# Sixteen start places instead of one for the moving operand of a split float32 matmul

## The reference

```python
h = rmsnorm(r, mix_pre_g)
z = h @ w_in + b_in                       # q, k, v | f_logit | u | g_attn, g_pool
attn = forgetting_attention(q, k, v, logf)
pool = multiscale_pool(u, pool_w, pool_scale)
m = sigmoid(g_attn) * (attn @ w_attn_o) + sigmoid(g_pool) * (pool @ w_pool_o)
r = r + rmsnorm(m @ w_out, mix_post_g)
h = rmsnorm(r, ffn_pre_g)
a = causal_dwconv(h @ w_up, conv_w, conv_b)      # width 3, 2 x 5632 channels
gate, val = split(a)
r = r + rmsnorm((gelu(gate) * val) @ w_down, ffn_post_g)
return r[:, 16:]
```

## Time and profile before

| | |
|---|---|
| time, median of 3 runs | 2045.64 us (2044.01 to 2048.0) |
| the profiled execution: its own time | 2047.04 us |
| its span, first to last instruction | 2045.2 us |
| TensorE, matmuls | 2004.3 us, 98% |
| TensorE, weight loads | 1914.3 us, 94% |
| VectorE | 1288.3 us, 63% |
| ScalarE | 987.0 us, 48% |
| GpSimd | 139.7 us, 7% |
| mean granted TensorE clock | 0.988 |

### The profile page before, as it was taken

The page is one execution under the profiler, slowest core; times in us unless marked ns, Lnnn a source line. Parts: engine busy times, 40 slices in busy tenths (PEclk is TensorE's granted clock), DMA queues, the critical chain, the costliest instruction groups (busy, mean ns, idle before and its releaser), DMA issues.

```text
span 2045.2 us, 39382 instructions
## 1 busy us (share of the span) xinstructions
PE 2004.3 (98%) x15326; PEld 1914.3 (94%) x15326; DVE 1288.3 (63%) x1668; ACT 987.0 (48%) x1434; POOL 139.7 (7%) x148
## 2 busy tenths in 40 slices
PE   6999999999999999999999999999999999999998
PEld 4999999999999999999999999999999999988886
DVE  6766878775677544444447753776776677665545
ACT  3334355565645444444445444644444445444444
POOL 0000000000002000000004211000010000000000
PEclk8899999999999999999999999999999999999999
DMA  9986866565545666554544555366556655665554
GB/s 355 346 299 192 295 219 214 177 202 169 163 160 169 178 175 174 166 154 144 147 150 147 195 196 164 114 203 183 169 177 199 188 174 177 210 202 192 194 187 143
DMA packets 188103, 391.75 MB, mean 192 GB/s; under 512 B 11955, under 2 KB 17632, under 8 KB 185568
## 3 DMA queue, kind: packets, MB, share of 16 engines
q1 hardware_dynamic: 186992, 388.03, 59.2%
q10 hardware_dynamic: 1024, 2.51, 0.4%
HBM read 388.39 MB, written 2.10 MB: 191 GB/s over the span
## 4 chain that ended last, share of the span: by engine, by line
PE 91%; DVE 4%; DMA 2%; ACT 1%; issue 1%; SPq 1%; DVEq 0%; ACTq 0%
PE acc L833 21%; PE acc L835 20%; PE acc L834 20%; PE psum_y L834 2%; PE psum_x L834 2%; PE psum_y L835 2%; PE psum_x L835 2%; PE psum_x L833 2%; PE psum_y L833 2%; PE acc L1253 2%; PE acc L1255 2%; PE acc L1254 2%; DMA ada_w<-in_w_ada 1%; DVE w_lo L1851 1%; PE psum_y L1253 1%; PE psum_x L1253 1%
## 5 line engine op out<-in xcount | busy, mean ns | idle before, releaser
L1851 DVE TENSOR_TENSOR w_lo<-raw,w_hi 128x1024 fp32r<-128x1024 f32 (+1 forms) x644 | 810.6, 1272 | 634.5 <-ACT w_hi L1317 632.0
L1317 ACT ACTIVATE w_hi<-raw 128x1024 fp32r<-128x1024 f32 (+1 forms) x644 | 671.0, 1050 | 783.2 <-PE acc L835 514.6
L833 PE MATMUL acc<-act_hi,w_lo 128*128 128x258 f32 (+2 forms) x3424 | 977.1, 285 | 6.8 <-DVE act_lo L1845 1.4
L834 PE MATMUL acc<-act_lo,w_hi 128*128 128x258 f32 (+2 forms) x3424 | 965.5, 282 | 0.0
L835 PE MATMUL acc<-act_hi,w_hi 128*128 128x258 f32 (+2 forms) x3424 | 965.3, 282 | 0.0
L833 PEld LDWEIGHTS acc<-act_hi,w_lo 128*128 128x128 f32 x3424 | 648.4, 189 | 15.7 <-issue 10.6
L834 PEld LDWEIGHTS acc<-act_lo,w_hi 128*128 128x128 f32 x3424 | 648.7, 189 | 0.6 <-issue 0.5
L835 PEld LDWEIGHTS acc<-act_hi,w_hi 128*128 128x128 f32 x3424 | 648.4, 189 | 0.0
L833 PE MATMUL psum_x<-act_hi,w_lo 128*128 128x258 f32 x352 | 99.3, 282 | 0.0
L835 PE MATMUL psum_y<-act_hi,w_hi 128*128 128x258 f32 x352 | 99.1, 281 | 0.0
L834 PE MATMUL psum_y<-act_lo,w_hi 128*128 128x258 f32 x352 | 99.1, 281 | 0.0
(11 more groups left out here) (326 smaller groups left out, 2270.5 us busy)
## 6 DMA issues: line engine op xcount, KB each, us to landing
raw<-in_w_in SPq DMA_DIRECT2D x272, 512.0 KB, 3.7
raw<-in_w_ffn_up SPq DMA_DIRECT2D x176, 512.0 KB, 4.5
raw<-in_w_ffn_down SPq DMA_DIRECT2D x88, 512.0 KB, 3.6
ada_w<-in_w_ada SPq DMA_DIRECT2D x64, 512.0 KB, 9.8
raw<-in_w_out SPq DMA_DIRECT2D x64, 512.0 KB, 4.0
ada_x<-in_w_ada SPq DMA_DIRECT2D x16, 1024.0 KB, 5.7
raw<-in_w_attn_o SPq DMA_DIRECT2D x16, 512.0 KB, 3.7
raw<-in_w_pool_o SPq DMA_DIRECT2D x16, 512.0 KB, 4.6
```

The lines of the kernel that those rows point to most:

```text
L833: pe.matmul(out, w_lo, a_hi, start=c == 0, stop=False)
L834: pe.matmul(out, w_hi, a_lo, start=False, stop=False)
L1317: act.activation(M.hi[s][:, 0:job.width], M.raw[s][:, 0:job.width], ACT.Copy).then_inc(M.hi_ready[s], 1)
L1851: dve.tensor_tensor(M.lo[s][:, 0:job.width], M.raw[s][:, 0:job.width], M.hi[s][:, 0:job.width].bitcast(FP32), ALU.subtract).then_inc(M.lo_ ...
```

## The change

The distance between the chunks of `act2_hi` and `act2_lo` becomes 323 columns, 1292 bytes, where it was 320 columns, 1280 bytes. The tensors keep their places and their size of 16 x 320 columns; the last chunk ends at column 5117. All readers (the jobs) and writers (`hi2_of`, `part2_hi`, `part2_lo`) of these chunks use the new distance. Chunk 0 stays where it was.

```diff
 PITCH = 320
+STEP = 323
...
     def act2(k, c0, n):
-        return M.act2_hi[:, PITCH * k + c0:PITCH * k + c0 + n], M.act2_lo[:, PITCH * k + c0:PITCH * k + c0 + n]
+        return M.act2_hi[:, STEP * k + c0:STEP * k + c0 + n], M.act2_lo[:, STEP * k + c0:STEP * k + c0 + n]
...
     def hi2_of(k, n):
-        return M.act2_hi[:, PITCH * k + ROWS - n:PITCH * k + ROWS]
+        return M.act2_hi[:, STEP * k + ROWS - n:STEP * k + ROWS]
...
-    part2_hi = lambda k, n: M.act2_hi[:, PITCH * k + ROWS - n:PITCH * k + ROWS].bitcast(FP32)
-    part2_lo = lambda k, n: M.act2_lo[:, PITCH * k + ROWS - n:PITCH * k + ROWS]
+    part2_hi = lambda k, n: M.act2_hi[:, STEP * k + ROWS - n:STEP * k + ROWS].bitcast(FP32)
+    part2_lo = lambda k, n: M.act2_lo[:, STEP * k + ROWS - n:STEP * k + ROWS]
```

## The result

The changed kernel takes 2053.39 us (median of 8 executions, 2049.06 to 2057.15), the kernel before 2046.22 us (8 executions, 2043.50 to 2052.86). The ratio is 1.003 with a 95% interval of 1.0015 to 1.0044: slower, by 7.2 us between the medians, which is small but clear of the noise. The forecast was 2055.5.

What follows compares the result with a forecast made beforehand. TensorE's matmul count times start-to-start pace was taken to bound the second block. 6.8 us (258 columns) plus 3.1 us (272 columns) gave 9.9 us, so 2055.5 us against the 2045.64 median; 8-in-10 range 2037 to 2072.

Steps and rivals of the forecast that it cites:

- Step 1: ScalarE's and VectorE's writes of the high and low chunks: no change; at most 2.8 us of ScalarE, hidden behind TensorE.
- Step 2: 258-column matmuls (g2, pool_w, pool_o, out2, up): 120.2 ns as in attn_o, 1.1 more on 6192 matmuls, 6.8 us.
- Step 3: 272-column matmuls: 126.0 ns from attn_o's surplus; qkv2 pays 2.7 ns on 1152 matmuls, 3.1 us; u2 and f2 nothing.
- Step 4: Everything behind TensorE's panels: ScalarE, VectorE and DMAs wait or start slightly later; nothing added or given back.
- Rival 1: Start place of TensorE's moving operand doesn't matter; nothing changes, 2045.6 us; chance 0.20.
- The formula that the prediction quotes: Matmul spacing of N/2.4 + 2.5 ns, no start place: 110.0 ns at 258 columns, where 119.0 was measured.
- Rival 2: Matmul starts inside a 16-byte piece of memory cost one more piece, 1.7 ns: 5.0 us, 2050.6 us; chance 0.13.
- Rival 3: Matmuls of odd chunks pay a whole step, 4.9 ns on 4272 matmuls: 20.9 us, 2066.6 us; chance 0.14.
- Rival 4: Faster: some odd chunks' 258-column matmuls run near 114.1 ns, gaining 8.5 us (2037) or 17 us (2028.6); chance 0.17.

Runs made afterwards that it cites:

- one-place panels: Kernel before, but each of up's panels 2 to 21 reads all its 258-column chunks from one column, differing by panel: 116.7 to 122.2 ns a matmul.
- short panels: Kernel before, single panels of up cut to 240 columns read at column 14 and 192 at column 0: 113.4 and 111.7 ns a matmul.

## Why the prediction was right

- **What bounds the kernel.** Right: matmul starts set the second block's time, and nearly all of the 7.0 us are in their pace. The picture under it, columns divided by the clock plus a surplus, doesn't hold: 192 and 240 columns go no quicker than about 112 ns, and at column 0 the step from 256 to 258 columns is 3.0 or 7.5 ns, depending on the level, not 0.8.
- **Step 1, the writers.** Right: ScalarE's medians are 404 and 501 ns (403 and 500 in the earlier trace rows), VectorE's 481 in both.
- **Step 2, 258 columns.** The direction and the mean hold, the size was at least 0.3 ns too large: 0.8 more in `up`, 0.6 in `pool_o` and 0.5 in `g2`, not 1.1, so about 4.3 us in place of 6.8. `attn_o`'s eight places, with high and low apart, were a fair sample but not this one; the mean over single places gives 119.9 or, with column 15, 119.6, beside 119.9 and 119.6 measured. The claim that no even place goes below 119.0 was wrong: column 10 runs at 117.8.
- **Step 3, 272 columns.** Right in the number, 126.0 predicted and 125.9 measured, but partly by luck: it was borrowed from a surplus at another length, and the 126.6 of `u2` that stood for it is the slower level of the old place, which ten of eleven profiles don't show in `u2`. For the same reason the zero for `u2` and `f2` holds only against the profiled execution; against the others it is 1.1 us. The runs give a better reason for `qkv2`: the old place, in its usual level, was among the three quickest of sixteen.
- **Step 4.** Right: nothing given back or added.
- **Rival 1** (the place doesn't matter) is refuted by the one-place panels. The formula that the prediction quotes from the Trainium skill ("TensorE: Matmul & The Clock Gate", "Back-to-back issue gap") is given there for an isolated matmul; for a stream of pairs of weight load and matmul, as here, the same section says that both set the spacing. The short panels fit that, though no run separates the two. **Rival 2** is refuted for 16-byte pieces: columns 0, 4 and 8 are 123.3, 126.6 and 125.4 at 272 columns. The Trainium skill ("SBUF — State Buffer", "Door 1: The DMA port swizzle") states cachelines of 16 bytes and a penalty for each access that crosses to a new one. That may hold for what it states, but it doesn't order these paces. **Rival 3** falls with the odd columns' mean and with the odd chunks in the changed kernel, 0.2 ns above the even ones. **Rival 4** was the wrong way for this change, but half of its idea is true: column 14 is not the best place, and single odd ones are quicker (3 by 1.2 ns, 7 by 2.3 in one of its levels, 15 by 3.5).

So the change is slower because the start places set the pace, and it trades one place that was better than the average for something near the average over all. That the places set it, stage by stage, is shown; that the new pace is an average of prices that belong to the single places is only roughly so. What a place's levels come from is open. Many settled paces are close to simple multiples of the 6.67 ns that 16 columns take at 2.4 GHz (115.6 is 17 1/3 of them, 116.7 is 17.5, 120.0 is 18, 123.3 is 18.5, 126.7 is 19), but `up`'s own 119.05 is 17.86 and not among them. That reads of moving and stationary operands wait for each other in some fixed round would be one explanation; it was not shown.

## What to carry to other kernels

When TensorE is the bound with back-to-back float32 passes, take the pace from start to start, panel by panel. A surplus over columns divided by the clock isn't by itself an address question, since here 192 columns still took 111.7 ns; what changed with the address were a few ns on top of that. Look for late starts too, since the level can change there, and compare several profiles before a pace goes into a sum. Spreading starts gave about the average, not the best: try one place per panel in a single run, take the quick ones that stay quick over a whole job, and time them, since the same place can have a second level. Here one column's shift of the late chunks was worth 0.8%.

## What the runs showed of the hardware

- The same matmul stream with the same addresses settles at different paces from one execution to the next and within one panel, and where the change was seen it fell on a start that came 0.18 to 0.46 us after the one before: 256 columns at 113.3 or 117.8 ns, 258 at column 14 at 119.0 or 120.0, 258 at column 7 at 116.7 or 120.0, 272 at column 0 at 123.3 or 126.7.
- With a weight load for each matmul, fewer columns stop paying below 256: 240 columns take 113.4 ns and 192 take 111.7, at a granted clock of 1.00.
- More columns can be free: 258 columns at column 0 take 120.8 ns, 264 take 120.2; 270 take 124.5, 272 take 123.4.
- Moving the input chunks of the late jobs by 4 bytes changed `up`'s pace from 119.0 to 115.8 ns.
